# ScalarE copies the turned exponentials of both maps of a pair out of PSUM, VectorE none of them

## The reference, cut to what matters

```
# sparse attention of block 1 (8 heads, 128 queries at a time)
s = jnp.einsum('bqhd,bqkd->bhqk', qb, k_sel) * scale
s = jnp.where(valid[:, None], s, -jnp.inf)
p = jax.nn.softmax(s, axis=-1)
return jnp.einsum('bhqk,bqkd->bqhd', p, v_sel)

# latent attention of block 2 (16 heads)
sc = (jnp.einsum('bqhd,bkhd->bhqk', qn, k_nope)
      + jnp.einsum('bqhr,bkr->bhqk', qr, k_rope)) * scale
sc = jnp.where(mask[None, None], sc, -jnp.inf)
p = jax.nn.softmax(sc, axis=-1)
return jnp.einsum('bhqk,bkhd->bqhd', p, v)
```

## Time and profile before

| | us |
|---|---|
| runs of the kernel before | 2413.04, 2414.85, 2414.76 (median 2414.76) |
| the profiled execution, its own time | 2414.19 |
| its span, from first to last instruction | 2412.9 |
| TensorE busy | 2294.3 (95%) |
| VectorE busy | 1398.7 (58%) |
| ScalarE busy | 1065.1 (44%) |
| mean granted TensorE clock | 0.98 of full speed |

### The profile page before, as it was taken

How to read it: one execution, slowest core, us unless ns; L and a number is a source line. 1 busy time by engine, 2 the same in 40 slices (tenths; PEclk the granted TensorE clock), 3 DMA queues, 4 the chain that set the end, 5 groups by cost and what they waited for, 6 DMA issues and landing times.

```text
span 2412.9 us, 26313 instructions
## 1 busy us (share of the span) xinstructions
PE 2294.3 (95%) x10768; PEld 1862.3 (77%) x10768; DVE 1398.7 (58%) x1903; ACT 1065.1 (44%) x1471; POOL 0.7 (0%) x5
## 2 busy tenths in 40 slices
PE   4999988898999999999998999999999999999998
PEld 2676767777788888888887878888888888888886
DVE  1459998786665464554555555454544554554554
ACT  2433444444344444434444555555444444444443
POOL 0000000000000000000000000000000000000000
PEclk8999999998999999999999999999999999999999
DMA  8988677593776575556554645454556555556553
GB/s 306 335 319 297 232 259 277 191 349 122 264 261 241 192 251 189 190 191 193 191 191 134 219 149 160 144 167 146 184 192 195 188 192 192 190 182 195 184 191 140
DMA packets 255455, 505.69 MB, mean 210 GB/s; under 512 B 9077, under 2 KB 19662, under 8 KB 254182
## 3 DMA queue, kind: packets, MB, share of 16 engines
q1 hardware_dynamic: 255334, 504.00, 62.0%
HBM read 499.77 MB, written 4.19 MB: 209 GB/s over the span
## 4 chain that ended last, share of the span: by engine, by line
PE 86%; DVE 7%; DMA 3%; ACT 2%; issue 1%; SPq 0%; DVEq 0%; ACTq 0%
PE bank L579 27%; PE bank L581 26%; PE bank L580 26%; DVE wlo L1656 2%; DVE acc L1639 2%; PE bank L595 2%; DMA raw<-in_w_in_dram 2%; PE bank L663 1%; ACT whi L1046 1%; DMA raw<-in_w_ada_dram 1%; PE bank L533 1%; PE bank L603 1%; DVE x L1708 0%; PE bank L686 0%; PE bank L666 0%
## 5 line engine op out<-in xcount | busy, mean ns | idle before, releaser
L1656 DVE TENSOR_TENSOR wlo<-raw,whi 128x1024 fp32r<-128x1024 f32 (+2 forms) x760 | 910.0, 1204 | 874.0 <-ACT whi L1046 873.6
L1046 ACT ACTIVATE whi<-raw 128x1024 fp32r<-128x1024 f32 (+2 forms) x760 | 790.5, 1044 | 1055.0 <-PE bank L581 971.8
L579 PE MATMUL bank<-whi,Ahi 128*128 128x512 f32 (+2 forms) x2304 | 914.0, 397 | 33.0 <-DVE wlo L1656 21.8
L580 PE MATMUL bank<-wlo,Ahi 128*128 128x512 f32 (+2 forms) x2304 | 897.8, 390 | 0.0
L581 PE MATMUL bank<-whi,Alo 128*128 128x512 f32 (+2 forms) x2304 | 897.5, 390 | 0.0
L579 PEld LDWEIGHTS bank<-whi,Ahi 128*128 128x128 f32 x2304 | 438.5, 190 | 136.1 <-DVE wlo L1656 32.8
L581 PEld LDWEIGHTS bank<-whi,Alo 128*128 128x128 f32 x2304 | 437.8, 190 | 90.8
L580 PEld LDWEIGHTS bank<-wlo,Ahi 128*128 128x128 f32 x2304 | 439.1, 191 | 83.8
L1639 DVE SCALAR_TENSOR_TENSOR acc<-raw,cs,acc 128x512 f32<-128x512 f32 x224 | 153.3, 744 | 0.0
L579 PE MATMUL bank<-whi,Fhi 128*128 128x512 f32 x352 | 137.7, 391 | 0.0
L581 PE MATMUL bank<-whi,Flo 128*128 128x512 f32 x352 | 137.0, 389 | 0.0
(11 more groups left out here) (291 smaller groups left out, 1347.4 us busy)
## 6 DMA issues: line engine op xcount, KB each, us to landing
raw<-in_w_in_dram SPq DMA_DIRECT2D x156, 1024.0 KB, 5.0
raw<-in_w_ada_dram SPq DMA_DIRECT2D x96, 1024.0 KB, 5.4
raw<-in_w_gate_dram SPq DMA_DIRECT2D x44, 1024.0 KB, 5.1
raw<-in_w_up_dram SPq DMA_DIRECT2D x44, 1024.0 KB, 5.1
raw<-in_w_down_dram SPq DMA_DIRECT2D x44, 1024.0 KB, 5.0
raw<-in_w_o_dram SPq DMA_DIRECT2D x16, 1024.0 KB, 5.1
raw<-in_w_o_mla_dram SPq DMA_DIRECT2D x16, 1024.0 KB, 4.9
raw<-in_w_o_conv_dram SPq DMA_DIRECT2D x16, 1024.0 KB, 5.0
```

The lines of the kernel that those rows point to most:

```text
L579: pe.matmul(o, a_hi, w_hi, start=beg, stop=False)
L580: pe.matmul(o, a_hi, w_lo, start=False, stop=False)
L1046: act.activation(m.whi[:, i % NHL, :, 0:n], m.raw[:, c % NRAW, 2 * h:2 * h + 2, 0:n], ACT.Copy).then_inc(m.s_hi, 1)
L1656: dve.tensor_tensor(m.wlo[:, i % NHL, :, 0:n], m.raw[:, c % NRAW, 2 * h:2 * h + 2, 0:n], m.whi[:, i % NHL, :, 0:n].bitcast(F32), ALU.subtr ...
```

## The change

In the sparse and in the latent attention, ScalarE's step gets a loop over both maps, and VectorE's step loses its copy. VectorE still steps through the same number of steps and counts the same bank uses. Nothing changes for the differential heads, where the loop has one turn. The names `ex` and `k.use` are the counters of bank uses.

```diff
@@ ScalarE, attention
             if n:
                 need.wait_ge(m.filled[b1], pv)
-            copy_out(ln.ET[:, 0:384], b0, ex[0], m.bank[b0][:, 0:384])
+            for mm, b in enumerate(ln.bank[0:nm]):
+                copy_out(ln.ET[:, 384 * mm:384 * mm + 384], b, ex[mm], m.bank[b][:, 0:384])
@@ ScalarE, mla_pair
         for b in (4, 5):
             need.wait_ge(m.filled[b], ex[b - 4])
-        copy_out(ln.ET[:, 0:384], 4, ex[0], m.bank[4][:, 0:384])
+        for mm in range(2):
+            copy_out(ln.ET[:, 384 * mm:384 * mm + 384], 4 + mm, ex[mm], m.bank[4 + mm][:, 0:384])
@@ VectorE, attention
-            ex = [k.use(b) for b in ln.bank[0:nm]]
-            yield
-            if nm == 2:
-                need.wait_ge(m.filled[b1], ex[1])
-                dve.tensor_copy(ln.ET[:, 384:768], m.bank[b1][:, 0:384]).then_inc(m.freed[b1], 1)
+            for b in ln.bank[0:nm]:
+                k.use(b)
+            yield
@@ VectorE, mla_pair
-        ex = k.use(4), k.use(5)
-        yield
-        need.wait_ge(m.filled[5], ex[1])
-        dve.tensor_copy(ln.ET[:, 384:768], m.bank[5][:, 0:384]).then_inc(m.freed[5], 1)
+        k.use(4), k.use(5)
+        yield
```

## The result

The changed kernel takes 2404.06 us (median of five runs, 2403.54 to 2406.76), the kernel before 2414.76 us (five runs beside them, 2413.04 to 2415.31). The ratio is 0.9963, with a 95% interval of [0.9952, 0.9974]: faster by 0.37%. In a second set of runs the same kernel took 2403.75 us against 2414.19, ratio 0.9957 [0.9944, 0.9969]. The forecast was 2402.8 us, its range 2399.5 to 2408.5.

What follows compares the result with a forecast made beforehand. The prediction took TensorE, busy for 95% of the span, to bound the kernel, with 13.5 us of idling that ended with a VectorE copy. It summed 2414.19 - 7.2 - 2.6 - 1.6 = 2402.8 us, range 2399.5 to 2408.5.

Steps and rivals of the forecast that it cites:

- Which waits, and what ends them: Before the weighing, seven latent waits (10.9 us) and two sparse (2.6 us) end with VectorE's copy, queued late.
- A copy on ScalarE: Second copy starts 0.37 us after the first and takes 0.49; both ready after 0.86 us, TensorE 0.1 us later.
- The seven latent pairs: Weighing in seven latent pairs starts 1.03 us earlier each, 7.2 us in all; bounds 6.8 to 7.6.
- The sparse pairs: Waits of 0.71 us in the first and 1.90 us in the fourth pair go: 2.6 us; bounds 0 to 2.6.
- The clock: Behind the fourth sparse pair it stays at 2.4 GHz once the idling goes: 1.6 us; bounds -1.6 to +1.6.
- Nothing added: ScalarE's next high part starts up to 0.37 us later in 12 places, hidden by 5.6 us of lead: 0.
- signs that were to show the prediction wrong: Latent `wlo` wait, weighing over 1.0 us after first copy, or new 350–460 us wait as long as the removed one.
- The forecasts of busy time: VectorE falls by 12 x 0.55 = 6.6 us; ScalarE rises by 12 x 0.49 = 5.9 us less overlap.
- nothing: Rival: the wait's name is wrong and another semaphore held the weighing; about 2414 us, chance 0.05.
- slower: Rival: ScalarE's list becomes the limit, added copies holding up high parts; 2420.1 us, chance 0.03.
- Only the latent part: Rival: time won in the sparse stretch is spent before the next late addition or load; 2407.0 us, chance 0.12.
- The clock gives nothing: Rival: the clock falls again at 471 us or elsewhere; 2404.4 us, chance 0.20.

Runs made afterwards that it cites:

- latent_alone: Kernel before with the change in the eight latent pairs only, the sparse attention keeping VectorE's copy; 2404.91 us, ratio 0.9963.
- sparse_alone: Kernel before with the change in the four sparse pairs only, the latent attention keeping VectorE's copy; 2412.35 us, ratio 0.9989.
- third_copy: Changed kernel with one more ScalarE copy, which nothing reads, ahead of the two in each latent pair; 2407.23 us, ratio 0.997.
- last_sparse_undone: Changed kernel with VectorE's copy of map 1 back in the fourth sparse pair alone; 2404.66 us, ratio 0.9957.
- scalar_early: Changed kernel with both ScalarE copies of the latent pairs one step earlier, right behind the transposes; 2401.49 us, ratio 0.9951.
- split_early: Changed kernel with both latent copies one step earlier, map 0 on ScalarE and map 1 on VectorE; 2399.83 us, ratio 0.9941.
- vector_early: Changed kernel with VectorE copying map 1 of the latent pairs one step earlier, ScalarE's map 0 at its old place; 2404.6 us, ratio 0.9961.

## Why the prediction was right, step by step

**Which waits, and what ends them: right.** The seven latent waits shrank and the two sparse ones went, and nothing else in the latent stretch changed.

**A copy on ScalarE: right in the copy, short in the handover.** Forecast: both maps ready 0.86 us after the start of the first, TensorE 0.10 us later. Measured: 0.87 us, and 0.15 us later (1433.88 - 1432.86 - 0.87), the upper end of my bounds. I had taken the middle between a weight load that followed a copy by 0.05 us and a matmul that followed one by 0.15; what the sum needed was the matmul. The page "ScalarE: Activation LUTs" of the Trainium skill, section "What ACT_TABLE_LOAD costs", gives an estimate of 0.92 us for two copies; the measurement decides, 0.87.

**The seven latent pairs: 7.2 forecast, 6.8 measured** (283.12 - 276.33, and 10.9 - 4.1 of waits), at the lower end of 6.8 to 7.6. The 0.4 us are the 0.05 us of handover, seven times. The waits that were left had been forecast as 3.7 us and are 4.1, for the same reason. The eighth pair gave nothing, as forecast.

**The sparse pairs: both waits went, and the clock took one of them back.** Measured from the first sparse turning, the fourth pair's weighing came at 470.36 - 343.90 = 126.46 us before and at 467.49 - 343.12 = 124.37 us after: 2.1 us for both waits, where 2.6 were expected. The first pair's gain was won and given back. Its weighing started 0.9 us sooner, and so did everything up to the scores of a differential head in lane b (line 663, `qT_b`), 64.6 us on instead of 65.5. But 6 us later the lead was gone. TensorE in the kernel before:

```profile
409.42 0.93 PE L663 MATMUL bank<-qT_b 64*128 64x256 f32 x4 [3.65 <-DVE modT L1620]
...
415.10 1.03 PE L595 MATMUL bank<-const,P 128*128 128x128 f32 x8
```

and in the kernel after:

```profile
407.73 1.22 PE L663 MATMUL bank<-qT_b 64*128 64x256 f32 x4 [3.66 <-DVE modT L1622]
...
414.31 1.03 PE L595 MATMUL bank<-const,P 128*128 128x128 f32 x8
```

From line 663 to line 595 it took 415.10 - 409.42 = 5.68 us before and 414.31 - 407.73 = 6.58 us after, for the same matmuls and without a wait between them. The windows say why. Before (the one from 410 to 412 us, with 0.50, is in the earlier trace rows):

```profile
408.00:410.00 2.00, 0.58 (x4) 0.30 (x4) 2.00 (x4) 0.00 (x0) 0.00 (x0) 0.94 1.03 378
...
412.00:414.00 2.00, 2.00 (x8) 1.58 (x7) 1.16 (x5) 0.00 (x0) 0.00 (x0) 0.71 0.98 350
```

And after:

```profile
405.00:407.00 2.00, 0.00 (x0) 0.00 (x0) 1.90 (x4) 0.16 (x1) 0.00 (x0) 0.80 1.01 384
407.00:409.00 2.00, 1.27 (x6) 0.63 (x6) 1.80 (x3) 0.00 (x0) 0.00 (x0) 0.50 1.04 403
409.00:411.00 2.00, 2.00 (x10) 1.49 (x10) 0.56 (x3) 0.00 (x0) 0.00 (x0) 0.50 1.04 354
411.00:413.00 2.00, 2.00 (x6) 1.52 (x6) 0.77 (x3) 0.00 (x0) 0.00 (x0) 0.50 1.03 400
```

Before, the clock fell to the 1.2 GHz level when TensorE had begun again after the idle time of 3.65 us, and stayed there for 3.4 us (added up from windows of half a microsecond). After, it had fallen inside the same idle time and stayed there for 6.8 us, to about the same place in the work. latent_alone, which has the first pair as before, has 3.4 us there; all eight profiles with the first pair changed have 6.8 us. sparse_alone gives the lead back at the same place (from 409.27 to 415.94 us, 6.67). In before and latent_alone TensorE reaches the fifth weighing 90.54 and 90.62 us after the first turning; in seven of the eight others it is 90.54 to 90.65 us, in the eighth (third_copy) 91.67. So the lead is lost in all eight, and the longer low clock is what took it. Why it lasts longer there is not settled: no experiment took that idle time away.

What the fourth pair gave was 2.1 us: 1.90 of named idling and 0.2 more, as below.

**The clock: 1.6 us forecast, 1.7 us at the place it was forecast for, 0.8 us in the stretch.** From the fourth weighing to the turn of line 595 it was 5.78 us before (476.14 - 470.36) and 4.11 us after (471.60 - 467.49):

```profile
471.60 1.03 PE L595 MATMUL bank<-const,P 128*128 128x128 f32 x8
```

The size was right. The reason given for it, the 1.90 us of idling in front, is not shown: last_sparse_undone had this idle time and no fall, and the fall can as well go with the change of the first pair. And against the 1.7 us stand the 0.9 us that the longer low clock at 407 us cost, a part of what the prediction had as its lower bound, "a fall elsewhere in its place". So in the prediction's own terms the sparse waits gave 0.9 + 2.1 = 3.0 us, 0.4 more than forecast, and the clock 1.7 - 0.9 = 0.8 us, half of what was forecast. That the two came out near 4.2 us together is partly luck.

**Nothing added: right.** No wait for `wlo` beyond the 0.2 us that the kernel before had, and no wait on a DMA. scalar_early shows how near that was: with the copies one step earlier, the high part of one more unit stands behind them, and TensorE waited for its low part behind each of the seven pairs. The 5.6 us of lead that I had read belong to the unit after it. Two of the signs that were to show the prediction wrong did appear, and neither bears on the mechanism. The weighing started 1.02 us after the first copy in the first pair, where more than 1.0 was to count; the limit was set too tight, since 0.86 us and the handover's own upper bound of 0.15 already make 1.01. And TensorE has a new named wait in the sparse stretch, 1.4 us for `Ex_b` at 425 us, longer than the 0.71 us removed. The turning behind it starts 82.36 us after the first one in both kernels, and latent_alone has this wait too, with its sparse pairs as before. In the kernel before the clock was 0.50 from 420 to 423 us, and TensorE spent the time on slower matmuls.

**The sum.** Forecast 7.2 + 2.6 + 1.6 = 11.4 us, traced 6.8 + 2.1 + 1.7 = 10.6 us; the medians differ by 10.7 us. The 0.8 us that are missing are 0.4 of handover in the latent pairs and 0.8 of clock, less 0.4 that the sparse waits gave beyond their named length. The forecasts of busy time were too large: VectorE fell by 5.2 us and not 6.6, ScalarE rose by 3.9 and not 5.9; a copy that overlaps its neighbour adds only its distance, 12 x 0.37 = 4.4 us at most on ScalarE.

Of the rivals, "nothing" and "slower" are excluded by the interval. "Only the latent part" (2407.0) is excluded for the profiled executions by the table, and not by the interval of the totals. "The clock gives nothing" (2404.4) is not excluded: the medians, 2404.06 and 2403.75 us, lie nearer to it than to 2402.8, and the 0.8 us that the clock gave in the trace lie half way between the two.

## What to carry to other kernels

A wait that names a short copy should be read in that engine's own list: here the copy took 0.55 us and stood 1.2 us behind a weight preparation, and an earlier place in the same engine's list served even better. Moving it to the other engine won 6.8 us there; leaving it on its engine one step earlier won 9.8. Moving both copies one step earlier, on both engines, won 5.9 us beyond the change, and piling the earlier copies on one engine only 2.1. A gain in front of a long idle time may not last past it: follow the new start to the next fall of the clock, and compare distances between the same instructions of both traces before a gain is counted. And a fall of the clock that goes away with a change needs a run that takes the supposed cause away alone, before it is put down to it.

## What the runs showed that was not expected

- A wait costs TensorE more than its named idle time. Between after and split_early 4.1 us of waits in seven places went, and the latent pairs became 276.33 - 270.46 = 5.9 us shorter: (5.9 - 4.1) / 7 = 0.25 us for each. The second pair shows the parts. Matmuls in front start 0.17 us apart but are listed with 0.34 us, and the idle time counts only from that modelled end; it leaves out 0.16 us. The first weighing matmul then takes 0.46 us in place of 0.38, 0.08 us more. scalar_early fits: it is 3.8 us longer than split_early, of which 2.0 are named waits in seven places, so again 0.25 us for each. The change itself did not win these 0.25 us in the latent pairs, since all seven waits stayed, only shorter; it did in the sparse ones, 0.9 us for a wait of 0.71 and 2.1 for one of 1.90 (2.0 in last_sparse_undone).
- This cost can be there with no wait named at all. In vector_early 2.8 us of named waits went and the latent pairs gained 3.0 us, hardly more: six pairs still start their weighing right behind ScalarE's copy. The weight load waits for it, the first matmul takes 0.49 us, and each of these pairs takes 38.36 us from one turning to the next, against 38.15 in split_early, where the load of 1469.14 us starts together with the last matmul in front of it. The second pair in vector_early:

```profile
1476.95 0.30 PEld L686 LDWEIGHTS bank<-kvb,G 128*128 128x128 f32 x2 [0.24 <-ACT G L1068]
1476.95 0.49 PE L686 MATMUL bank<-kvb,G 128*128 128x128 f32 x2
```

- Four falls of the granted clock to the 1.2 GHz level follow TensorE waits of 3.65, 2.48, 2.33 and 1.90 us in the sparse stretch of the kernel before, while 2.70 us in the first latent pair were followed by none. Of the three profiles with the wait of 1.90 us, two had a fall behind it.
- Stretches that no edit touches vary between single executions by up to 5.5 us (343.1 to 348.6) and 2.8 us (943.0 to 945.8). The second goes with the clock: it takes up to 943.8 us in the profiles in which the clock was at the 1.2 GHz level for 21 to 24 us of it, and 944.9 us or more in those with 27 to 31 us. The first doesn't go with it: 343.1 us with 48 us at that level, 344.6 with 28.
